# ScalarE scales keys and values of a chunked recurrence, and 24 gathered row sets change their stage

## The chip, the cores and the metric

The kernel runs on one core of one Trainium2 chip. The metric is the device time of one execution in microseconds. Three timed runs of the kernel before gave 5598.96, 5606.19 and 5611.48 us; the median is 5606.19.

## The reference

One layer of a hybrid trunk for 128 context tokens and 512 latent tokens, model width 2048, all in float32:

```python
h = rmsnorm(x, norm_mix) * (1 + sc1) + sh1          # modulated by m = silu(cond) @ w_mod + b_mod
q, k, v = silu(short_conv(h @ w_in[qkv]))           # 8 heads of 128; q and k of unit norm
# gated delta rule, forward and backward in time:
# S_t = exp(g_t) (I - beta_t k_t k_t^T) S_{t-1} + beta_t k_t v_t^T ;  o_t = S_t^T q_t / sqrt(dk)
p_a = (rmsnorm(o) * silu(z)) @ w_branch_a
p_b = chunk_spatial_gate(u, vg) @ w_branch_b        # one 128x128 position mix per channel group
x = x + gt1 * ((sigmoid(ga) * p_a + sigmoid(gb) * p_b) @ w_out)
h2 = rmsnorm(x, norm_ffn) * (1 + sc2) + sh2
# PEER: 8 heads, 2 x 128 sub-keys, top 16 of each half
s = (h2 @ w_query) . sub_keys
sv, si = top_k(s, 16)
cand = sv[0][:, None] + sv[1][None, :]              # 16 x 16 sums
best, pos = top_k(cand, 16); gates = softmax(best)
y = sum_e gelu(h2 . expert_u[idx_e]) * gate_e * expert_v[idx_e]      # 128 experts for each token
x = x + gt2 * y;  y_out = rmsnorm(x, norm_final)
```

The latent scans start from a cached state; the context's final states are an output.

## The kernel before, in words

Tokens go in five blocks of 128, one partition each: block 0 is the context, 1 to 4 the latent. The program is a row of stages, each a block with one instruction list per engine, and a barrier between them. `modulation` and `mixer_input` come first. Then the context goes through `qkv`, `deltanet`, `branches`, `merge`, `output_projection`, `expert_input` and `scores`; the four latent blocks go together through `qkv` and `deltanet`; then the second group (latent block 1) and the last group (blocks 2 to 4) each go through `branches` to `scores`; `experts` is last. Weights come in tiles of 1 MB over SyncE's queue into a ring of four.

**Row sets.** Each token has 128 chosen experts. The kernel takes them one place at a time: a row set is one row of 8 KB for each of the 128 tokens of a block, gathered by one indirect DMA of GpSimd (L316), 1 MB in all. A block needs 128 sets of `peer_u` and then 128 of `peer_v`; five blocks need 1280. VectorE uses a set in one instruction on 128x2048: a multiply and sum for `peer_u` (L363), a multiply and add into the block's total for `peer_v` (L368). Between both ScalarE applies Gelu once (`gelu_rows`). The context's sets are free for use once its `scores` are done, so they are spread over the stages that follow. `take(t, counts, slots)` names how many sets lie behind each step of a stage and in how many buffers; `use_rows` is VectorE's part, `gather_rows` and `gather_until` GpSimd's, which wait until a set's buffer has been used; `gather_ahead` issues the first three sets of the stage that follows. What is left is done by `experts` with six buffers, and nothing else is computed there. Before, 451 sets lie ahead of `experts` and 829 in it.

**The recurrence (`deltanet`).** A batch is one block of 128 tokens in one direction for all 8 heads: two batches for the context, eight for the latent. A triangular system is inverted by doubling in levels 1 to 6. In each level TensorE multiplies the masked matrix (L902), ScalarE copies the product from PSUM (L1107), TensorE multiplies again (L908), and VectorE adds the result into the inverse (L1038, L1040). GpSimd makes the mask product for each level (L838) in two buffers. Between levels VectorE also makes `kbe`, `kd` and `vn`, the transposed keys and values times a factor per token and head (L1051, L1053, L1056), after level 4 and 5 the decay terms of the next batch (L1001, L1013). TensorE puts products for the next batch behind its levels 4 and 5 (L892). After level 6 VectorE runs `begin` for the next batch (L1021 to L1030), then takes the outputs (L1072, L1074) and sums the state (L1077), for which TensorE waits before the next batch's transposes of the keys (L897). In the latent recurrence 4 row sets go with each of the first seven batches in three buffers: one after level 2, one after level 3, two after level 6.

**`branches`.** For each of 8 heads TensorE projects a z tile (L216) and transposes the head's normalised output (L1186), which GpSimd scales first (L1166) and then issues the gathers behind that head. Then come 2 x 4 tiles of `vg` (L1224), with most of the sets behind them, and 8 of `u`.

**`output_projection`.** 4 x 3 banks of products (L1500), each multiplied by VectorE (L1532) with sets behind it, and added to x by GpSimd (L1549). For the last group it also closes the context's block (L1512 to L1520) ahead of the first product.

**`scores`.** 16 tiles of queries (L216) and their scores (L1662). VectorE finds the top 16 of each (`top`), forms the 256 sums (L1725), finds their top 16 (L1732 to L1744) and picks the keys (`route`). All sets lie ahead of the first tile.

## Time and profile before

| | us |
|---|---|
| median of three runs | 5606.19 |
| profiled execution, its time | 5607.62 |
| its span | 5605.8 |
| VectorE busy | 3904.2 (70%) |
| TensorE matmul busy | 3073.4 (55%) |
| GpSimd busy | 2940.7 (52%) |
| ScalarE busy | 519.0 (9%) |
| DMA, mean rate | 338 GB/s, 1892.52 MB |

Busy time is summed over the whole span; each stage has its own limit, so the share of an engine over the span says little of one stage. PE is TensorE, PEld its weight loads, DVE is VectorE, ACT ScalarE, POOL GpSimd, SP SyncE. An entry in brackets behind an instruction is its engine's idle time just before it, and who ended it.

### The profile page before, as it was taken

How to read it: one execution, taken by the hardware profiler on the slowest of the kernel's cores; microseconds unless marked ns; L12 is line 12 of the kernel's file. 1: busy time of each engine (PE TensorE's matmuls, PEld its weight loads, DVE VectorE, ACT ScalarE, POOL GpSimd, SP SyncE). 2: the span in 40 equal slices, each digit the busy share in tenths (PEclk: the TensorE clock that was granted, in tenths of full speed). 3: DMA queues.
4: the chain of work that ended last, by engine and by line, in shares of the span. 5: the costliest groups of instructions: out<-in, count | busy, mean ns of one | idle time of the engine just before them, and what ended most of it. 6: DMA issues, size and time to landing. Idle time of an engine off the chain costs nothing. (4 is left out here: it accounts for less than half of the span.)

```text
span 5605.8 us, 41938 instructions
## 1 busy us (share of the span) xinstructions
PE 3073.4 (55%) x16118; PEld 2149.6 (38%) x16118; DVE 3904.2 (70%) x4330; ACT 519.0 (9%) x857; POOL 2940.7 (52%) x1532
## 2 busy tenths in 40 slices
PE   5989988998997886898998967000000000000000
PEld 2787955448996875455554444000000000000000
DVE  1340027976664436665776679899999999999998
ACT  1521002422221000000000000000000000000000
POOL 0131003745552210544543520888888888888887
PEclk7999989999999998999999988555555555555555
DMA  9819878973227996897999851999999999999998
GB/s 388 345 56 344 320 300 321 395 316 110 80 76 302 391 388 239 336 358 310 420 420 404 358 225 61 422 420 422 422 419 421 419 421 420 420 408 422 422 422 363
DMA packets 272942, 1892.52 MB, mean 338 GB/s; under 512 B 31780, under 2 KB 36132, under 8 KB 49511
## 3 DMA queue, kind: packets, MB, share of 16 engines
q0 software_dynamic: 194560, 1409.51, 61.5%
q1 hardware_dynamic: 71558, 440.26, 20.1%
q10 hardware_dynamic: 6624, 40.07, 1.8%
q8 instruction: 128, 2.10, 0.1%
q14 instruction: 72, 0.58, 0.0%
HBM read 1870.78 MB, written 18.94 MB: 337 GB/s over the span
## 5 line engine op out<-in xcount | busy, mean ns | idle before, releaser
L216 PE MATMUL ps<-arena_sb 128*128 128x128 f32 (+2 forms) x9216 | 1889.4, 367 | 128.4 <-PEq L1634 32.6
L316 POOL DMA_INDIRECT arena_sb<-peer_v,arena_sb x640 | 1303.6, 2037 | 840.5 <-DVE arena_sb L368 426.0
L368 DVE SCALAR_TENSOR_TENSOR arena_sb<-arena_sb 128x2048 f32<-128x2048 f32 x635 | 1497.8, 2359 | 193.7 <-DMA arena_sb<-peer_v,arena_sb 120.6
L216 PEld LDWEIGHTS ps<-arena_sb 128*128 128x128 f32 x9216 | 1328.9, 196 | 706.8 <-issue 324.4
L363 DVE CUSTOM_DVE_ANT_0 arena_sb<-arena_sb 128x2048 f32<-128x2048 f32 x640 | 1475.3, 2319 | 176.6 <-DMA arena_sb<-peer_u,arena_sb 176.3
L316 POOL DMA_INDIRECT arena_sb<-peer_u,arena_sb x640 | 1258.8, 1967 | 459.2 <-DVE arena_sb L363 266.9
L262 POOL DMA_DIRECT2D arena_sb<-w_mod x64 | 34.8, 544 | 617.3 <-PE ps L223 485.9
L838 POOL TENSOR_TENSOR arena_sb<-arena_sb 128x1024 f32<-128x1024 f32 x60 | 185.1, 3095 | 217.3 <-ACT arena_sb L1098 165.0
L1500 PE MATMUL ps<-arena_sb 128*128 128x512 f32 x640 | 279.4, 599 | 30.7 <-PEq L1354 30.0
L1419 DVE TENSOR_TENSOR arena_sb<-ps,arena_sb 128x128 f32<-128x128 f32 (+1 forms) x96 | 35.2, 378 | 350.4 <-PE ps L216 350.1
L908 PE MATMUL ps<-arena_sb 128*128 128x64 f32 x1760 | 206.4, 275 | 0.0
L908 PEld LDWEIGHTS ps<-arena_sb 128*128 128x128 f32 x1760 | 203.6, 194 | 0.0
L1500 PEld LDWEIGHTS ps<-arena_sb 128*128 128x128 f32 x640 | 122.7, 192 | 186.7 <-issue 184.3
L902 PE MATMUL ps<-arena_sb 128*128 128x128 f32 x1280 | 176.5, 292 | 10.8 <-DVE arena_sb L1030 9.4
L902 PEld LDWEIGHTS ps<-arena_sb 128*128 128x128 f32 x1280 | 163.9, 204 | 14.4 <-issue 9.8
L223 PE MATMUL ps<-arena_sb,scond_sb 128*32 128x512 f32 x768 | 129.5, 711 | 56.4 <-ACT scond_sb L436 30.1
L1224 PE MATMUL ps<-arena_sb 128*128 128x512 f32 x320 | 143.6, 607 | 11.4 <-DMA arena_sb<-w_vg 11.4
L1038 DVE TENSOR_TENSOR arena_sb<-arena_sb,ps 128x256 f32<-128x256 f32 x100 | 42.0, 420 | 146.8 <-PE ps L908 146.7
L1549 POOL TENSOR_TENSOR arena_sb<-arena_sb 128x512 f32<-128x512 f32 x20 | 41.9, 2093 | 194.6 <-DVE arena_sb L1532 194.4
L659 DVE TENSOR_SCALAR arena_sb<-ps,cw_sb 128x128 f32<-128x128 f32 (+1 forms) x48 | 26.4, 551 | 139.4 <-PE ps L216 138.3
L1841 ACT ACTIVATE ps<-arena_sb 128x2048 f32<-128x2048 f32 x4 | 7.5, 1882 | 1139.1 <-DVE arena_sb L1854 1139.1
L1403 ACT ACTIVATE arena_sb<-ps 128x128 f32<-128x128 f32 (+1 forms) x96 | 33.3, 348 | 803.1 <-PE ps L216 663.9
(222 smaller groups left out, 2299.9 us busy)
## 6 DMA issues: line engine op xcount, KB each, us to landing
arena_sb<-w_mod POOLq DMA_DIRECT2D x64, 1024.0 KB, 8.2
arena_sb<-w_qkv SPq DMA_DIRECT2D x48, 1024.0 KB
arena_sb<-w_ga SPq DMA_DIRECT2D x48, 1024.0 KB
arena_sb<-w_gb SPq DMA_DIRECT2D x48, 1024.0 KB
arena_sb<-w_out SPq DMA_DIRECT2D x48, 1024.0 KB
arena_sb<-w_query SPq DMA_DIRECT2D x48, 1024.0 KB
arena_sb<-w_mod SPq DMA_DIRECT2D x32, 1024.0 KB
arena_sb<-w_z SPq DMA_DIRECT2D x24, 1024.0 KB
```

The lines of the kernel that those rows point to most:

```text
L216: mm = pe.matmul(out, weights[:, k * P:(k + 1) * P], x[:, k, :], start=(k == 0), stop=(k == chunks - 1))
L223: mm = pe.matmul(out[32 * j:32 * j + 32, :], t.scond[:, k + j, :], weights[:, j * COL:(j + 1) * COL], start=start, stop=stop, tile_positio ...
L316: nc.gpsimd.indirect_dma_start(slot, None, a["peer_v" if adds else "peer_u"], bass.IndirectOffsetOnAxis(ap=g.index[:, p:p + 1], axis=0)).t ...
L363: nc.vector.tensor_tensor_reduce(rows, rows, total, 1.0, 0.0, ALU.mult, ALU.add, g.dots[:, p:p + 1]).then_inc(t.rows_used, 1)
L368: nc.vector.scalar_tensor_tensor(out=total, in0=rows, scalar=g.weight[:, p:p + 1], in1=total, op0=ALU.mult, op1=ALU.add).then_inc(t.rows_u ...
L838: nc.gpsimd.tensor_tensor(lev[:, k % 2], mt, over(nmask[:, 1 - r, k], H), ALU.mult).then_inc(s["level_masked"], 1)
L902: mm = pe.matmul(bank(out + u)[:, h % 4], lhs[:, h], rhs[:, h], start=True, stop=True)
L908: mm = pe.matmul(compact(bank(2 + u), k, side)[:, h % 4], lhs[:, h], changed(rhs, k, second)[:, h], start=True, stop=True)
L1038: nc.vector.tensor_tensor(cols, cols, compact(bank(2 + u), k, 1), ALU.add)
L1224: mm = pe.matmul(t.ps[:, 4 * c + b, :], h[:, k, b * P:(b + 1) * P], tile_slot(t, H + 4 * c + kq)[:, kk * COL:(kk + 1) * COL], start=(k == ...
L1500: mm = pe.matmul(t.ps[:, 4 * (c % 2) + b, :], merged[:, k, b * P:(b + 1) * P], tile_slot(t, 4 * c + kq)[:, kk * COL:(kk + 1) * COL], start ...
L1549: nc.gpsimd.tensor_tensor(cols, cols, part[:, b], ALU.add).then_inc(part_added, 1)
```

## The change

In `deltanet` the three multiplies by a factor per token and head leave VectorE; ScalarE makes each as 8 copies of 128x128 from PSUM with a scale operand, after the same level. TensorE waits for `kbe` by a semaphore of its own. The latent batches have 7 row sets each: two after levels 1, 2 and 3, one after level 5, none after level 6. GpSimd issues one gather after each of the masks 3 to 6 and three at the batch's end. In `branches` of the second and last group GpSimd issues gathers at the stage's start and then those behind head n-1 once it has scaled head n. In `output_projection` of the last group the closing of the context's block is a function called after the second column, and no set lies behind the last three products. In all `scores` stages the 16 x 16 sums become 4 x 16 and 12 x 4 (a sum of place i and j can only be among the best 16 if (i+1)(j+1) is at most 16), and the place is worked out in float steps; in the last group 10 sets are added between the heads. Lists of `take`: the last `branches` 76 to 75 sets, the last `output_projection` 38 to 32, the last `scores` 10 to 20, the latent recurrence 28 to 49; 475 sets lie ahead of `experts` and 805 in it.

```diff
+FULL = 4
+FEW = 4
+PAIRS = FULL * 16 + (16 - FULL) * FEW
@@ deltanet
-    behind = take(t, [4] * loads, 3, 6)
+    behind = take(t, [7] * loads, 3, 6)
@@ deltanet, gpsimd
                 for k in range(3, LEVELS):
                     masked(n, at[0], k)
-                    if n < loads and k >= 5:
-                        gather_until(pool, nc, t, a, min(behind[n].start + k - 1, t.rows))
+                    if n < loads:
+                        gather_until(pool, nc, t, a, min(behind[n].start + k + 1, t.rows))
...
-                    gather_until(pool, nc, t, a, min(behind[n].start + 7, t.rows))
+                    gather_until(pool, nc, t, a, min(behind[n].stop + 3, t.rows))
@@ deltanet, tensor
             def finish(n, r, j, b):
+                pe.wait_ge(s["kbe_done"], n + 1)
@@ deltanet, vector
                     level(n, r, k)
-                    if k == 1:
-                        dve.wait_ge(s["ktok_ps"], n + 1)
-                        nc.vector.tensor_tensor(kbe, banks(6), wide(gate(t.beg, r, b, 0, 8), P), ALU.mult)
-                    elif k == 2:
-                        nc.vector.tensor_tensor(kd, banks(6), wide(tail, P), ALU.mult)
-                    elif k == 3:
-                        dve.wait_ge(s["vtok_ps"], n + 1)
-                        nc.vector.tensor_tensor(vn, banks(0), wide(gate(t.beta, r, b, 0, 8), P),
-                                                ALU.mult).then_inc(s["tok_read"], 1)
-                    elif n + 1 < 2 * nb and k == 4:
+                    if n + 1 < 2 * nb and k == 4:
+                        dve.wait_ge(s["tok_read"], n + 1)
                         differences(n + 1, *order[n + 1])
...
-                    if n < loads and k in (2, 3):
-                        use_rows(dve, nc, t, behind[n][k - 2:k - 1])
-                if n < loads:
-                    use_rows(dve, nc, t, behind[n][2:4])
+                    if n < loads and k in (1, 2, 3, 5):
+                        use_rows(dve, nc, t, behind[n][6:7] if k == 5 else behind[n][2 * k - 2:2 * k])
@@ deltanet, scalar
+            def scaled(out, first, scales):
+                for h in range(H):
+                    ins = nc.scalar.activation(out[:, h], bank(first + h // 4)[:, h % 4], ACT.Copy,
+                                               scale=scales[:, h:h + 1])
+                return ins
...
+                    if k == 1:
+                        act.wait_ge(s["ktok_ps"], n + 1)
+                        scaled(kbe, 6, beg).then_inc(s["kbe_done"], 1)
+                    elif k == 2:
+                        scaled(kd, 6, tail)
+                    elif k == 3:
+                        act.wait_ge(s["vtok_ps"], n + 1)
+                        scaled(vn, 0, beta).then_inc(s["tok_read"], 1)
+                    if n < loads and k in (1, 2, 3, 5):
+                        gelu_rows(act, nc, t, behind[n][6:7] if k == 5 else behind[n][2 * k - 2:2 * k])
@@ branches
-                  [4, 3] * (H // 2) + [27] + [3] * (H - 1) + [0], 4)
+                  [3] * H + [30] + [3] * (H - 1) + [0], 4)
@@ branches, gpsimd
+            if not ctx:
+                gather_rows(pool, nc, t, a, [range(t.held, t.held)], 0)
             pool.wait_ge(o_step, 2 * nb + 2)
             for n in range(H):
...
-                else:
-                    gather_rows(pool, nc, t, a, behind, n)
+                elif n:
+                    gather_rows(pool, nc, t, a, behind, n - 1)
@@ output_projection
-    behind = take(t, [4, 3] * 5 + [3, 0] if last else [0] * (4 * nb), 4)
+    behind = take(t, [4, 4, 4, 4, 4, 4, 3, 3, 2, 0, 0, 0] if last else [0] * (4 * nb), 4)
@@ output_projection, vector
-            if last:
+            def finish_context():
...
                     use_rows(dve, nc, t, behind[nb * c + b])
+                if last and c == 1:
+                    finish_context()
@@ scores
-    behind = take(t, [0 if ctx else 10 if nb == 3 else 4], 4 if nb == 3 else 3)
+    behind = take(t, [10, 2, 1, 2, 1, 2, 1, 1, 0] if nb == 3 else [0 if ctx else 4] + [0] * H, 4 if nb == 3 else 3)
@@ scores, route
-                step.step(nc.vector.tensor_tensor(
-                    sums.rearrange("p b (i j) -> p b i j", i=TOPK),
-                    value[0].unsqueeze(3).to_broadcast([P, nb, TOPK, TOPK]),
-                    value[1].unsqueeze(2).to_broadcast([P, nb, TOPK, TOPK]), ALU.add))
+                for lo, hi, w, o in ((0, FULL, TOPK, 0), (FULL, TOPK, FEW, FULL * TOPK)):
+                    n = hi - lo
+                    ins = nc.vector.tensor_tensor(
+                        sums[:, :, o:o + n * w].rearrange("p b (i j) -> p b i j", i=n),
+                        value[0][:, :, lo:hi].unsqueeze(3).to_broadcast([P, nb, n, w]),
+                        value[1][:, :, 0:w].unsqueeze(2).to_broadcast([P, nb, n, w]), ALU.add)
+                step.step(ins)
...
+                step.step(nc.vector.tensor_copy(place_f, place))
+                at, by16, by4 = (place_f[:, u * n5:(u + 1) * n5] for u in range(3))
+                first, second = spot_f[:, 0:n5], spot_f[:, n5:2 * n5]
+                step.step(nc.vector.scalar_tensor_tensor(out=first, in0=by4, scalar=float(FULL - FULL * TOPK // FEW),
+                                                         in1=by16, op0=ALU.add, op1=ALU.max))
+                for out, w in ((down[0], TOPK), (down[1], FEW)):
+                    ins = nc.vector.scalar_tensor_tensor(out=out, in0=first, scalar=-float(w), in1=at, op0=ALU.mult,
+                                                         op1=ALU.add)
+                step.step(ins)
+                step.step(nc.vector.scalar_tensor_tensor(out=second, in0=down[1], scalar=float(FULL * FEW - FULL * TOPK),
+                                                         in1=down[0], op0=ALU.add, op1=ALU.max))
...
             for h in range(H):
                 top(2 * h)
                 top(2 * h + 1)
                 route(h)
+                use_rows(dve, nc, t, behind[h + 1])
```

## Rows read from the trace of the kernel before

**Rows 1.** The page: mean busy share of the DMA engines in 40 slices.

```profile
DMA  9819878973227996897999851999999999999998
```

**Rows 2.** Windows by stage: us, busy time (instructions) of each engine, clock, DMA share, GB/s.

```profile
1263.60:1719.70 456.10, 419.25 (x3520) 413.95 (x3520) 296.68 (x520) 111.13 (x192) 227.83 (x100) 0.95 0.23 82
1719.90:1854.20 134.30, 101.52 (x616) 79.09 (x616) 65.16 (x52) 15.33 (x28) 33.81 (x35) 0.95 1.00 416
2241.60:2542.90 301.30, 280.55 (x824) 154.18 (x824) 201.82 (x114) 18.26 (x29) 153.65 (x84) 0.96 0.87 342
3300.60:3496.80 196.20, 165.68 (x576) 101.79 (x575) 179.42 (x690) 9.65 (x18) 4.22 (x4) 0.93 0.25 91
3496.80:5605.80 2109.00, 0.00 (x0) 0.00 (x0) 1953.32 (x1236) 18.73 (x22) 1790.78 (x826) 0.50 1.00 416
```

**Rows 3.** Windows of the gathers (L316) alone in `experts`: GpSimd busy (instructions), clock, DMA.

```profile
4350.00:4900.00 550.00, 477.39 (x221) 0.50 1.01 420
```

**Rows 4.** Groups by line in the latent recurrence: busy us, mean ns, idle before.

```profile
L363 DVE CUSTOM_DVE_ANT_0 arena_sb<-arena_sb 128x2048 f32<-128x2048 f32 x28 | 64.8, 2333 | 0.0
...
L1056 DVE TENSOR_TENSOR arena_sb<-ps,beta_sb 128x1024 f32<-128x1024 f32 x8 | 9.7, 1218 | 0.0
```

**Rows 5.** TensorE in time order at a batch's start, context then latent, and one window.

```profile
352.92 1.09 PE L897 MATMUL ps<-ident_sb,arena_sb 128*128 128x128 f32 x8 [0.51 <-DVE arena_sb L1077]
353.84 1.95 PE L902 MATMUL ps<-arena_sb 128*128 128x128 f32 x16
...
1449.82 1.97 PE L897 MATMUL ps<-ident_sb,arena_sb 128*128 128x128 f32 x8 [3.74 <-DVE arena_sb L1077]
1451.58 3.62 PE L902 MATMUL ps<-arena_sb 128*128 128x128 f32 x16
...
1449.70:1455.00 5.30, 5.18 (x25) 5.18 (x25) 0.07 (x1) 0.60 (x1) 5.07 (x3) 0.50 0.51 206
```

**Rows 6.** VectorE and GpSimd in time order in a latent batch, and the gathers' landing.

```profile
1461.13 2.36 POOL L838 TENSOR_TENSOR arena_sb<-arena_sb 128x1024 f32<-128x1024 f32 x1 [3.50 <-PE ps L902]
1462.82 0.42 DVE L1038 TENSOR_TENSOR arena_sb<-arena_sb,ps 128x256 f32<-128x256 f32 x1 [1.85 <-PE ps L908]
...
1466.66 4.26 POOL L838 TENSOR_TENSOR arena_sb<-arena_sb 128x1024 f32<-128x1024 f32 x1 [3.17 <-PE ps L902]
...
arena_sb<-peer_u,arena_sb POOLq DMA_INDIRECT x28, 6.1
```

**Rows 7.** VectorE in time order: the state sums of the first and seventh latent batch.

```profile
1338.11 1.20 DVE L1077 TENSOR_TENSOR arena_sb<-arena_sb,ps 128x1024 f32<-128x1024 f32 x1
...
1672.23 1.21 DVE L1077 TENSOR_TENSOR arena_sb<-arena_sb,ps 128x1024 f32<-128x1024 f32 x1
```

**Rows 8.** Groups by line and form, ScalarE, whole span: instructions on 128x128.

```profile
L1690 ACT ACTIVATE arena_sb<-ps 128x128 f32<-128x128 f32 x32 | 8.9, 277 | 150.1 <-PE ps L216 150.1
...
L713 ACT ACTIVATE arena_sb<-ps,small_sb 128x128 f32<-128x128 f32 x16 | 5.9, 367 | 19.8 <-PE ps L600 19.8
```

**Rows 9.** Last `branches`: a wait (us in total, times, longest), and the first `vg` products.

```profile
PE ps L1186 <- POOL arena_sb L1166: 14.3, 5, 4.0
...
2349.64 50.79 PE L1224 MATMUL ps<-arena_sb 128*128 128x512 f32 x114
```

**Rows 10.** Last `output_projection` in time order: start, us, instruction.

```profile
3066.36 166.97 PE L1500 MATMUL ps<-arena_sb 128*128 128x512 f32 x384 [17.43 <-PEq L1354]
...
3248.92 0.68 DVE L1532 TENSOR_TENSOR arena_sb<-ps,arena_sb 128x512 f32<-128x512 f32 x1
...
3253.60 0.94 POOL L316 DMA_INDIRECT arena_sb<-peer_v,arena_sb  x1 [0.30 <-issue]
...
3263.87 0.17 DVE L1581 TENSOR_REDUCE stat_sb<-stat_sb 128x3 f32<-128x12 f32 x1 [14.27 <-PEq L1447]
```

**Rows 11.** Last `scores`, groups by line and form.

```profile
L1716 DVE MAX8 arena_sb<-arena_sb 128x8 f32<-128x128 f32 x48 | 10.9, 282 | 0.6
...
L1725 DVE TENSOR_TENSOR arena_sb<-arena_sb 128x768 f32<-128x768 f32 x8 | 7.7, 959 | 0.3
L1741 DVE MAX8 arena_sb<-arena_sb 128x8 f32<-128x256 f32 x24 | 8.6, 415 | 0.3
```

More of the change, by code:

```diff
@@ L1103, in _ @@
             for n in range(2 * nb):
+                r, _, b = order[n]
+                beg, beta = (x[:, g.first + b, 8 * r:8 * r + 8] for x in (t.beg, t.beta))
                 for k in range(1, LEVELS):
@@ L1486, in _ @@
                     gelu_rows(act, nc, t, behind[nb * c + b])
+                if last and c == 1:
+                    act.wait_ge(fin_step, 2)
+                    nc.scalar.activation(x_c, total, ACT.Square, accum_out=ss_c).then_inc(fin_root, 1)
+                    act.wait_ge(fin_step, 3)
+                    nc.scalar.activation(ss_c, ss_c, ACT.Sqrt).then_inc(fin_root, 1)
             act.wait_ge(norm_in, 48)
@@ L1534, in _ @@
                     use_rows(dve, nc, t, behind[nb * c + b])
+                if last and c == 1:
+                    finish_context()
                 if c == 2:
@@ L1616, in scores @@
     z = g.scratch
-    value = [z[:, u * n5:(u + 1) * n5].rearrange("p (b n) -> p b n", b=nb) for u in range(2)]
-    keyf = [z[:, (2 + u) * n5:(3 + u) * n5].rearrange("p (b n) -> p b n", b=nb) for u in range(2)]
-    where = z[:, 4 * n5:5 * n5].bitcast(U32).rearrange("p (b n) -> p b n", b=nb)
-    place = [z[:, (5 + u) * n5:(6 + u) * n5].bitcast(U32) for u in range(3)]
-    place_f = [z[:, (8 + u) * n5:(9 + u) * n5] for u in range(2)]
-    o = 10 * n5
-    sums = z[:, o:o + nb * 256].rearrange("p (b n) -> p b n", b=nb)
-    left = z[:, o + nb * 256:o + 2 * nb * 256].rearrange("p (b n) -> p b n", b=nb)
-    onehot = [z[:, o + (2 + u) * nb * 256:o + (3 + u) * nb * 256] for u in range(2)]
+    part_of = lambda i, w=1: z[:, i * n5:(i + w) * n5]
+    value = [part_of(u).rearrange("p (b n) -> p b n", b=nb) for u in range(2)]
+    where = part_of(2).bitcast(U32).rearrange("p (b n) -> p b n", b=nb)
+    place, place_f = part_of(3, 3).bitcast(U32), part_of(6, 3)
+    spot_f, down = part_of(9, 2), [part_of(11), part_of(12)]
+    keyf = [[part_of(13 + 2 * s + u).rearrange("p (b n) -> p b n", b=nb) for u in range(2)] for s in range(2)]
+    o = 17 * n5
+    sums = z[:, o:o + nb * PAIRS].rearrange("p (b n) -> p b n", b=nb)
+    left = z[:, o + nb * PAIRS:o + 2 * nb * PAIRS].rearrange("p (b n) -> p b n", b=nb)
+    onehot = z[:, o + 2 * nb * PAIRS:o + 2 * nb * (PAIRS + 256)]
     total = t.stat[:, 0:nb * H]
@@ L1652, in _ @@
             else:
-                gather_rows(pool, nc, t, a, behind, 0)
+                gather_rows(pool, nc, t, a, behind, H)
                 gather_ahead(pool, nc, t, a)
@@ L1690, in _ @@
                 nc.scalar.activation(query[n % 2], t.ps[:, n % 4, 0:nt], ACT.Copy).then_inc(query_done, 1)
+                if n % 2 and n > 4:
+                    gelu_rows(act, nc, t, behind[n // 2 - 1])
+            for rows in behind[H - 1:]:
+                gelu_rows(act, nc, t, rows)
             if ctx:
@@ L1720, in top @@
                 step.step(ins)
-                step.step(nc.vector.tensor_copy(keyf[u], where))
+                step.step(nc.vector.tensor_copy(keyf[n // 2 % 2][u], where))
             def route(h):
-                step.step(nc.vector.tensor_tensor(
-                    sums.rearrange("p b (i j) -> p b i j", i=TOPK),
-                    value[0].unsqueeze(3).to_broadcast([P, nb, TOPK, TOPK]),
-                    value[1].unsqueeze(2).to_broadcast([P, nb, TOPK, TOPK]), ALU.add))
+                for lo, hi, w, o in ((0, FULL, TOPK, 0), (FULL, TOPK, FEW, FULL * TOPK)):
[5 more added lines that the diff above has]
+                step.step(ins)
                 best = best_all[:, :, h, :]
-                spot = place[0].rearrange("p (b k) -> p b k", b=nb)
+                spot = place[:, 0:n5].rearrange("p (b k) -> p b k", b=nb)
                 for b in range(nb):
@@ L1745, in route @@
                 step.step(ins)
[L1746 to L1754 removed]
+                nc.vector.tensor_scalar(place[:, n5:2 * n5], place[:, 0:n5], 4, None, ALU.logical_shift_right)
```

30 lines of the change are left out of this document (12 added, 18 removed).

## The prediction

> **What bounds the kernel now.** I read the slices of the page first: over the last two fifths the DMA digits stand at 9 without a break, and before that they fall to 2 to 7 in places [rows 1]. The windows by stage say more [rows 2]. The last 2109 us (`experts`) hold no matmul and run at 416 GB/s with a DMA share of 1.00, VectorE 1953 us busy. What sets the pace there is the gather of row sets (128 rows of 8 KB, 1.0486 MB): 221 in 550 us of steady run at 420 GB/s [rows 3], 2.49 us each. VectorE takes 1953/829 = 2.36 us of that. So a row set used earlier gives back 2.49 us at the end, and the question for each earlier stage is what it pays. Those stages have other limits [rows 2]: the latent recurrence has TensorE 419 of 456 us busy with a DMA share of 0.23; `branches` of the last group 281 of 301; `scores` of the last group has VectorE 179 of 196 and DMA 0.25.
>
> **Row sets moved.** Summing the `take` lists (those of 128x1 stages are unchanged): recurrence 28 to 49, last `branches` 76 to 75, last `output_projection` 38 to 32, last `scores` 10 to 20. Net 24 sets leave `experts`: 24 x 2.49 = -59.8 us. The whole stage, its ends included, gives 2109/829 = 2.54, so the term lies between -59 and -61.
>
> **The recurrence.** Per batch VectorE loses three multiplies of 1.22 us and gains three row sets [rows 4]. Before, two sets lie at the batch's end, between level 6 and `begin`. TensorE waits there for the state sum: 3.74 us idle, then the clock stands at 0.50, 1.2 GHz, for some 5 us: 8 transposes take 1.97 us and level 1's first 16 products 3.62 [rows 5]. The context's batches have no sets there and show what it is like without: 0.51 us idle, 1.09 and 1.95 us for the same. So taking both sets away is worth 3.2 of idle time and 0.9 + 1.7 of slow products, 5.8 us a batch.
> What it costs: a level takes 5.5 us; between the adds of two levels VectorE has its multiply of 1.22 and 1.85 us idle [rows 4, 6], 3.1 in all, and some 0.8 more before TensorE wants the next columns: about 3.9. Two sets take 4.42, so TensorE slips 0.6 us a level. Beyond that there are two further prices. First, GpSimd's mask multiply takes 2.36 us alone and 4.26 beside a set [rows 6]; the two exclude each other. With two sets in a row the mask can go between them: VectorE's pair then takes 6.8 us and TensorE slips 2.9. The Trainium skill (SBUF — State Buffer, "SBUF: two separate sides") has the rule: a VectorE instruction with two SBUF inputs and a GpSimd one hold the shared port pair for a whole instruction, and the other is blocked; the 1.9 us added beside a set agree. By the rule each level pays the 2.9, by no contention the 0.6. Second, only three buffers: sets 0 to 2 are there, set 3 is issued behind mask 3 and once set 0 is used, and lands 6.1 us after issue [rows 6]. Following GpSimd's order from the state sum (0): set 3 issues at 10 to 12 and lands at 16 to 18 (wanted 15.5), set 4 lands at 22 (wanted 21), set 5 at 26 to 29 (wanted 23). Level 4's adds come at 28 to 31; two blocks of 16 products for the next batch (1.95 each, as level 1's) stand between level 4 and 5 and cover most. Level 6 then starts at 37.3 to 39.2 instead of 36.5 (33.7 without slips). A batch comes to 53.7 to 55.5 us against 55.7 (six periods between the ends of these state sums, 1339.31 to 1673.44 [rows 7]). I take 55.0: 7 batches x -0.7 = -5 us. Ends: -2.6 a batch (no contention, timely landings) and +3 (each landing 2 us later, another mask in the way): -18 to +20.
> ScalarE's 8 multiplies of 128x128 from PSUM: 277 ns as a plain one, 367 with a pointer operand [rows 8]; 8 x 0.367 = 2.9 us (at least 2.2, and 3.7 if the scale costs a second 90 ns). Between a level's copies and the next level's it is idle as long as a level less its two copies, 5.5 - 1.6 = 3.9 us. I count nothing; if that cover fails by x us, TensorE waits x three times a batch. The table load for Gelu falls here once: 3 us either way, and it leaves a later stage.
>
> **`branches` of the last group.** GpSimd scales head n+1 only after the gathers behind head n, and these wait for VectorE. TensorE waits 14.3 us for it in five places, and some tiles after a wait run slower; eight heads take from 2241.6 [rows 2] to 2349.6 [rows 9], 108 us. A tile without a wait takes 11.0 us with its transposes, as in `scores` (sixteen from 3287.9 to 3466). With the gathers one head behind, GpSimd has scaled a head some 12 us before it is wanted, VectorE's part being 0.6 + 3 x 2.45 = 8 us: 13.5 for the first tile at the slow clock + 7 x 11.0 + 0.5 = 91. DMA then carries 3 sets and a tile in 11 us, 381 GB/s, under 422 but near. I take -14 (ends -6 and -17). The three sets more behind the `vg` products (30) cost nothing: 30 x 2.45 = 73 us beside 117 us of TensorE. In the stage of the second group the early gather changes nothing: DMA share is 1.00 all through.
>
> **`output_projection` of the last group.** Products end at 3233.3, but VectorE, with sets behind each product, is at its last one at 3248.92; GpSimd then issues the three gathers ahead (last 3253.60) and the next stage starts at 3263.87 [rows 10]. In the change all sets lie behind the first nine products. VectorE, waiting for landings, does a set in 3.4 us here, so 12 sets from 3103 to 3145, 12 more to 3186, the moved closing of the context 11 us, 8 sets to 3223: just before the tenth product's 3226.5. The moved closing saves nothing where it was: its wait for loads from the ScalarE queue lay before the first product was ready. Last product at 3234, last gather 3239, next stage 9.3 us later as now, 3248.7: -15. Ends: -17, and -8 if VectorE arrives 7 us late.
>
> **`scores`.** Candidates fall from 256 to 112. A maximum takes 415 ns at 256 and 282 at 128, 1.04 ns an element, so 265 at 112 [rows 11]; I take the index search and the replacement at the same rate. Per head with three blocks that is 15 x -0.15, and -0.3 for the sums (336 elements for 768, in two instructions): -2.6 us. The index arithmetic goes from 4 small instructions (0.64 us) to 7: +0.75. 8 x -1.9 = -15. Ten sets more at 2.45: +24.5. VectorE is the one behind: TensorE's last product ends at 3466, the stage at 3496.8 [rows 2]. So +9 (ends +4 and +14). With one block the same is -0.1 a head: -1 for each of the two other stages, -2 together (ends -3 and +6, if the added steps wait longer).
>
> **Sum.** -59.8 - 5 - 14 - 15 + 9 - 2 = -86.8. The profiled execution took 5607.6 (span 5605.8 and 1.8 around it), so 5520.8; it lies 1.4 above the median of the runs, so 5519.
>
> **Rivals.** (a) The recurrence pays: every level gives the full contention and landings are late, +3 a batch. For it: 4.26 beside a set [rows 6]. Against: 3.9 us cover and the products between level 4 and 5. +20 instead of -5: 5544.
> (b) The two stage gains don't come, since DMA stands near its limit there: `branches` at 381 of 422 GB/s, and `output_projection` has fewer sets but denser. -6 and -8 instead of -14 and -15, and with it +14 in `scores`: 5539. Against: what VectorE waits for is set by the order of GpSimd's program, not by bytes.
> (c) It goes better: landings in time and 5.8 us a batch mostly kept, -18 for it, and -17 twice: 5501.
> (d) Slower than before: with three buffers the gathers become the batch's chain. Sets 3, 4, 5 and 6 each expose landing and use, 6.1 + 2.3 = 8.4 us, and since GpSimd sits in a gather's wait its masks come late too, so that nothing covers: 33.6 - 5.8 = +28 a batch, +195 for seven: 5519 + 5 + 195 = 5719. It decides from (86.8 - 5)/7 = 11.7 us a batch on. Against: no mask needs a set that needs that mask, and the sets wanted first have landed.
>
> **Numbers.** Forecast 0.60, (a) 0.16, (b) 0.13, (c) 0.08, (d) 0.03. What a measurement here can tell from no change is 0.2%, 11 us; same and slower lie only in (d) or several ends together: faster 0.95, same 0.02, slower 0.03. Range: all good ends give 5495, all bad ones but (d) 5572; 8 in 10 lie in 5492 to 5555.
>
> **What would show it.** In `experts` 805 sets and some 2049 us; if it isn't 60 shorter, the first term is wrong. In the latent recurrence: TensorE's idle before L897 under 1 us and the clock at 2.4 GHz there; waits of the second set of levels 2 and 3 for peer rows; a period of 54 to 56. If TensorE waits for ScalarE copies or for masks (POOL L838), my covers were wrong. In `branches` the 14 us wait for POOL gone and eight heads in 91 to 100 us. In `output_projection` the last product read within 1 us of 3233's counterpart. In `scores` 205 us. The forecast is wrong if the recurrence takes over 480 us, or if a stage between grows by what `experts` loses.

## The result, and the profile after

The changed kernel takes 5573.64 us (median of 4 runs, 5569.33 to 5587.77) beside 5607.51 for the kernel before (4 runs, 5598.96 to 5611.48): a ratio of 0.9946, 95% interval 0.9924 to 0.9968. It is faster, since the interval leaves out 1, but by 34 us and not by the forecast's 87; 5519 was 55 us too low and the range ended 19 us under the median. The profiled execution is the slowest of the four, 5587.77 (span 5585.9), so it lies 19.8 us under the profiled one of before, and the table accounts for that difference.

| stage, start to next start, us | before | after | change | forecast |
|---|---|---|---|---|
| latent recurrence | 456.3 | 505.6 | +49.3 | -5 |
| last `branches` | 310.6 | 308.5 | -2.0 | -14 |
| last `output_projection` | 197.5 | 184.6 | -13.0 | -15 |
| last `expert_input` and `scores` | 233.4 | 242.2 | +8.8 | +9 |
| the other two `scores` | 179.5 | 177.0 | -2.5 | -2 |
| `experts` | 2108.5 | 2047.5 | -61.0 | -59.8 |
| all others | 2119.0 | 2119.6 | +0.6 | 0 |

The same stages in the windows of the trace after (columns as in [rows 2]): recurrence, last `branches`, last `output_projection`, last `scores`, `experts`.

```profile
1263.80:1769.20 505.40, 452.14 (x3520) 445.70 (x3520) 352.48 (x520) 163.69 (x387) 270.69 (x121) 0.88 0.33 117
2287.90:2596.40 308.50, 276.13 (x825) 153.28 (x826) 197.89 (x133) 18.16 (x29) 146.69 (x83) 0.94 0.85 337
3111.60:3296.20 184.60, 166.42 (x384) 73.43 (x384) 94.92 (x50) 12.16 (x28) 86.73 (x44) 0.95 0.82 330
3334.50:3538.40 203.90, 165.72 (x576) 101.79 (x574) 186.74 (x724) 9.66 (x18) 20.29 (x14) 0.91 0.37 141
3538.40:5585.90 2047.50, 0.00 (x0) 0.00 (x0) 1896.66 (x1212) 18.73 (x22) 1739.91 (x802) 0.50 1.00 416
```

Beside [rows 2], TensorE's matmuls in the recurrence are the same 3520, but busy 452 us instead of 419, and the granted clock's mean is 0.88 instead of 0.95: the products themselves ran longer. That splits the 49 us: 33 are slower products, the other 16 more idle time (505.4 - 452.1 = 53.3 us beside 456.1 - 419.3 = 36.9). `experts` keeps its 416 GB/s and is shorter only by what it no longer does.

TensorE's idle time in the recurrence by what it waited for (us in total, times, longest), the kernel before and then the changed one:

```profile
PE ps L897 <- DVE arena_sb L1077: 26.2, 7, 3.7
```

```profile
PE ps L905 <- DVE arena_sb L1044: 25.9, 16, 4.5
PE ps L905 <- POOL arena_sb L841: 13.0, 2, 8.2
PE ps L900 <- DVE arena_sb L1071: 3.9, 7, 0.9
```

The wait for the state sum fell from 26.2 to 3.9 us as forecast. In its place came 25.9 us of waits for VectorE's adds (L1044) and 13.0 us for GpSimd's masks (L841), of which the kernel before had 0.7. The six periods between the ends of the first seven state sums are 57.2 to 65.1 us, 62.0 on the mean, against 55.7 before and 55.0 forecast; the stretch from the stage's start to the first of them grew from 75.7 to 88.8.

One latent batch of after, TensorE in time order, from the end of the batch before (start, us, instruction, idle before):

```profile
1469.68 1.09 PE L900 MATMUL ps<-ident_sb,arena_sb 128*128 128x128 f32 x8 [0.51 <-DVE arena_sb L1071]
1470.61 1.95 PE L905 MATMUL ps<-arena_sb 128*128 128x128 f32 x16
1472.40 3.74 PE L911 MATMUL ps<-arena_sb 128*128 128x64 f32 x32
1475.98 2.17 PE L905 MATMUL ps<-arena_sb 128*128 128x128 f32 x16
1477.98 3.68 PE L911 MATMUL ps<-arena_sb 128*128 128x64 f32 x32
1483.77 3.75 PE L905 MATMUL ps<-arena_sb 128*128 128x128 f32 x16 [2.10 <-DVE arena_sb L1044]
1487.32 6.93 PE L911 MATMUL ps<-arena_sb 128*128 128x64 f32 x32
```

VectorE and GpSimd in the same stretch:

```profile
1476.85 3.89 DVE L366 CUSTOM_DVE_ANT_0 arena_sb<-arena_sb 128x2048 f32<-128x2048 f32 x1
...
1480.67 2.28 DVE L366 CUSTOM_DVE_ANT_0 arena_sb<-arena_sb 128x2048 f32<-128x2048 f32 x1
...
1484.21 4.15 DVE L366 CUSTOM_DVE_ANT_0 arena_sb<-arena_sb 128x2048 f32<-128x2048 f32 x1
...
1488.71 5.04 DVE L366 CUSTOM_DVE_ANT_0 arena_sb<-arena_sb 128x2048 f32<-128x2048 f32 x1 [0.34 <-DMA arena_sb<-peer_u,arena_sb]
```

```profile
1476.23 2.36 POOL L841 TENSOR_TENSOR arena_sb<-arena_sb 128x1024 f32<-128x1024 f32 x1
1481.02 2.80 POOL L319 DMA_INDIRECT arena_sb<-peer_u,arena_sb  x1 [2.43 <-DVE arena_sb L366]
1483.82 2.38 POOL L841 TENSOR_TENSOR arena_sb<-arena_sb 128x1024 f32<-128x1024 f32 x1
1486.36 2.85 POOL L319 DMA_INDIRECT arena_sb<-peer_u,arena_sb  x1 [0.16 <-issue]
1489.23 2.36 POOL L841 TENSOR_TENSOR arena_sb<-arena_sb 128x1024 f32<-128x1024 f32 x1
```

The batch's start is as forecast: 0.51 us idle, transposes 1.09 and level 1's products 1.95, against 3.74, 1.97 and 3.62 in [rows 5]. Then come two sets in a row. Beside a mask (L841) a set takes 3.9 to 5.0 us instead of 2.3, and the gather's issue (L319) takes 2.8 us instead of 0.94 [rows 10] when it runs beside a set. TensorE waits 2.10 us for the adds (L1044) behind the second set, and what follows runs at half the clock: level 3's products take 3.75 and 6.93 us where level 1's take 1.95 and 3.74. The clock shows it, 1.00 in the window of levels 1 and 2 and 0.50 in that of level 3:

```profile
1470.00:1482.00 12.00, 11.67 (x104) 11.44 (x101) 6.57 (x7) 6.51 (x20) 9.48 (x6) 1.00 0.65 249
1483.80:1494.20 10.40, 10.40 (x48) 10.25 (x48) 10.06 (x8) 3.25 (x10) 10.05 (x5) 0.50 0.61 203
```

The longest wait for a mask, 8.20 us, has a cause of its own. It falls in the fifth batch, the first one of the backward direction, whose start state SyncE loads from memory once the last forward batch is done:

```profile
1530.42 0.38 SPq L825 DMA_DIRECT2D arena_sb<-state  x1
...
1541.19 2.69 POOL L862 TENSOR_TENSOR arena_sb<-arena_sb 128x1024 f32<-128x1024 f32 x1 [9.56 <-issue]
...
1550.63 3.79 PE L905 MATMUL ps<-arena_sb 128*128 128x128 f32 x16 [8.20 <-POOL arena_sb L841]
```

These 512 KB land 10.7 us after their issue, among the gathers of the batch's end (5.9 us in the kernel before). GpSimd's first multiply of the batch (L862) waits for them by the program, and its masks come behind that. The kernel before has the same load, but no wait of TensorE for a mask in this batch.

### The profile page after: what moved, and what is told of

Read it like the earlier page. It is cut to its first block and busy times, and to the rows that moved or that the text cites. A ratio compares the mean times of both kernels' runs of the same rounds, so it can differ in the third digit from the quotient of the medians.

```text
span 5585.9 us, 42233 instructions
## 1 busy us (share of the span) xinstructions
PE 3098.4 (55%) x16118; PEld 2175.9 (39%) x16118; DVE 3880.2 (69%) x4372; ACT 581.4 (10%) x1097; POOL 2930.9 (52%) x1532
## 5 line engine op out<-in xcount | busy, mean ns | idle before, releaser
L319 POOL DMA_INDIRECT arena_sb<-peer_v,arena_sb x640 | 1277.9, 1997 | 926.3 <-DVE arena_sb L371 556.1
L371 DVE SCALAR_TENSOR_TENSOR arena_sb<-arena_sb 128x2048 f32<-128x2048 f32 x635 | 1513.7, 2384 | 247.9 <-DMA arena_sb<-peer_v,arena_sb 178.0
L366 DVE CUSTOM_DVE_ANT_0 arena_sb<-arena_sb 128x2048 f32<-128x2048 f32 x640 | 1499.8, 2359 | 167.3 <-DMA arena_sb<-peer_u,arena_sb 166.6
L219 PEld LDWEIGHTS ps<-arena_sb 128*128 128x128 f32 x9216 | 1319.9, 194 | 716.5 <-issue 332.9
L319 POOL DMA_INDIRECT arena_sb<-peer_u,arena_sb x640 | 1291.8, 2018 | 480.0 <-DVE arena_sb L366 289.8
L841 POOL TENSOR_TENSOR arena_sb<-arena_sb 128x1024 f32<-128x1024 f32 x60 | 163.7, 2736 | 224.4 <-ACT arena_sb L1092 182.1
L911 PE MATMUL ps<-arena_sb 128*128 128x64 f32 x1760 | 227.4, 292 | 0.0
L911 PEld LDWEIGHTS ps<-arena_sb 128*128 128x128 f32 x1760 | 225.0, 210 | 0.0
L905 PE MATMUL ps<-arena_sb 128*128 128x128 f32 x1280 | 186.9, 304 | 49.6 <-DVE arena_sb L1044 25.9
L1515 PEld LDWEIGHTS ps<-arena_sb 128*128 128x128 f32 x640 | 122.8, 193 | 187.6 <-issue 184.5
L905 PEld LDWEIGHTS ps<-arena_sb 128*128 128x128 f32 x1280 | 173.1, 215 | 54.5 <-issue 38.6
L1549 DVE TENSOR_TENSOR arena_sb<-ps,arena_sb 128x512 f32<-128x512 f32 x20 | 13.8, 688 | 157.2 <-PE ps L1515 157.2
```

What stands on the lines that cost most here:

```text
L219: mm = pe.matmul(out, weights[:, k * P:(k + 1) * P], x[:, k, :], start=(k == 0), stop=(k == chunks - 1))
L319: nc.gpsimd.indirect_dma_start(slot, None, a["peer_v" if adds else "peer_u"], bass.IndirectOffsetOnAxis(ap=g.index[:, p:p + 1], axis=0)).t ...
L366: nc.vector.tensor_tensor_reduce(rows, rows, total, 1.0, 0.0, ALU.mult, ALU.add, g.dots[:, p:p + 1]).then_inc(t.rows_used, 1)
L371: nc.vector.scalar_tensor_tensor(out=total, in0=rows, scalar=g.weight[:, p:p + 1], in1=total, op0=ALU.mult, op1=ALU.add).then_inc(t.rows_u ...
L841: nc.gpsimd.tensor_tensor(lev[:, k % 2], mt, over(nmask[:, 1 - r, k], H), ALU.mult).then_inc(s["level_masked"], 1)
L905: mm = pe.matmul(bank(out + u)[:, h % 4], lhs[:, h], rhs[:, h], start=True, stop=True)
```

## The experiments

Each of these runs but e9 is one execution. They are compared by their stages, since two executions differ by some 10 us elsewhere (`modulation` alone took from 123 to 130 us). The recurrence itself repeats well: e8 has that of the changed kernel and took 504.8 us beside 505.6, e9 has that of e7 and took 463.1 beside 463.0. First the window of the latent recurrence of e1, e2, e3, e4, e5, e6, e7 and e10, in this order; the stage's length is the number before the comma.

```profile
1258.20:1715.70 457.50, 418.19 (x3520) 413.11 (x3520) 272.57 (x496) 160.67 (x385) 215.16 (x100) 0.95 0.23 81
```

```profile
1256.30:1684.40 428.10, 407.85 (x3520) 401.95 (x3520) 280.49 (x496) 160.84 (x384) 207.23 (x100) 0.98 0.25 87
```

```profile
1255.70:1721.90 466.20, 430.86 (x3520) 424.90 (x3520) 297.93 (x521) 163.56 (x388) 166.26 (x122) 0.93 0.35 127
```

```profile
1262.30:1758.20 495.90, 440.38 (x3520) 433.77 (x3520) 361.91 (x544) 114.48 (x196) 269.54 (x121) 0.91 0.34 119
```

```profile
1263.00:1749.00 486.00, 445.98 (x3744) 438.44 (x3744) 346.32 (x521) 164.29 (x388) 270.43 (x121) 0.96 0.34 122
```

```profile
1260.80:1710.00 449.20, 416.99 (x3520) 410.34 (x3520) 329.35 (x513) 165.96 (x387) 237.34 (x114) 0.96 0.34 116
```

```profile
1261.80:1724.80 463.00, 421.55 (x3520) 415.35 (x3520) 340.76 (x520) 165.07 (x387) 245.55 (x121) 0.95 0.37 128
```

```profile
1259.50:1723.30 463.80, 418.23 (x3520) 411.39 (x3520) 378.64 (x544) 116.31 (x196) 232.96 (x121) 0.96 0.36 128
```

**e1: ScalarE's scaling alone.** The changed kernel with four sets a batch, placed and gathered as before.

```diff
-    behind = take(t, [7] * loads, 3, 6)
+    behind = take(t, [4] * loads, 3, 6)
+    CUT = (0, 0, 1, 2, 2, 2, 4)
...
+    use_rows(dve, nc, t, behind[n][CUT[k - 1]:CUT[k]])
```

> The changed kernel, but the latent recurrence has its 4 row sets a batch where they were before (one after level 2, one after level 3, two after level 6) and GpSimd's gathers as before; ScalarE keeps the scaling. Recurrence before 456 us, changed 505. If the row sets' number and place make the 49 us (theories A and B below): 448 to 458 us, VectorE only relieved. If ScalarE's scaling makes them (theory C: its 24 short instructions delay the copies TensorE waits for): 480 us or more, with waits of TensorE for L1109 copies. Theory A: two sets in a row on VectorE and GpSimd's masks and gathers shut each other out for whole instructions, the levels slip, and TensorE's idle time drops its clock. Theory B: with three buffers the sets land late and VectorE waits for them.

5587.52 us; the recurrence takes 457.5 beside 456.3 before. Moving the scaling neither costs nor gains anything while the sets stand where they stood. The 49 us come with the sets' new number and places.

**e2: four sets, apart.** Against e1 (GpSimd's gathers follow, one behind each of the masks 3 to 6):

```diff
-    CUT = (0, 0, 1, 2, 2, 2, 4)
+    CUT = (0, 1, 2, 3, 3, 4, 4)
```

> As the run before, but the 4 sets of a batch go one after each of levels 1, 2, 3 and 5, none after level 6. A and B both expect that the 5.8 us a batch of idle and slow TensorE at the batch's start go; A takes back up to 0.8 us in each of three levels (set 2.3 + mask 2.35 against 3.9 us of cover), so 416 to 432 us for the recurrence (456 before); B nothing, 416. C: 480 or more. Fewer sets early (28 for 49) cost 21 x 2.49 = 52 us in experts.

5555.41 us, the recurrence 428.1, and five of the six periods between its first seven state sums are 50.8 us (the fourth is 53.9). With the clock at 0.98 and TensorE 408 of 428 us busy this is nearly TensorE's own time. Against e1 that is 29 us, 4.2 a batch: two sets of 2.3 us taken off the end of a batch, where nothing hid them. The forecast's gain of 5.8 a batch for this came to 4.5 in the periods (55.3 to 50.8).

**e3: the masks nearly taken away.** GpSimd multiplies only 8 of the 128 columns of each mask; the buffers are cleared once, so the rest is zero and most of the masked matrix is left out.

```diff
-                nc.gpsimd.tensor_tensor(lev[:, k % 2], mt, over(nmask[:, 1 - r, k], H),
+                nc.gpsimd.tensor_tensor(lev[:, k % 2, :, 0:8], mt[:, :, 0:8], over(nmask[:, 1 - r, k, 0:8], H),
                                         ALU.mult).then_inc(s["level_masked"], 1)
```

> The changed kernel with 7 sets, but each of GpSimd's mask products is made on 8 of 128 columns only (the rest of the buffer is cleared once), so the solve leaves most of its levels' mask out. Waits and order are unchanged. A: the sets on VectorE fall from 2.3 to 5.0 us back to 2.3 to 2.4 beside masks (gathers can still stretch one), 7 us a batch: recurrence 450 to 465 us, TensorE at the full clock in level 3 and 4. B: the landings stay where they are, sets wait longer instead: 495 to 505 us.

5541.06 us, the recurrence 466.2 (1 us over theory A's range): 39 of the 49 us are gone. The groups by line of e3's recurrence:

```profile
L366 DVE CUSTOM_DVE_ANT_0 arena_sb<-arena_sb 128x2048 f32<-128x2048 f32 x30 | 74.2, 2488 | 12.1 <-DMA arena_sb<-peer_u,arena_sb 12.1
L319 POOL DMA_INDIRECT arena_sb<-peer_u,arena_sb x30 | 44.5, 1484 | 17.8 <-DVE arena_sb L366 12.3 <-issue 5.1
...
L371 DVE SCALAR_TENSOR_TENSOR arena_sb<-arena_sb 128x2048 f32<-128x2048 f32 x18 | 42.3, 2349 | 11.0 <-DMA arena_sb<-peer_v,arena_sb 10.4
```

and of the changed kernel's:

```profile
L366 DVE CUSTOM_DVE_ANT_0 arena_sb<-arena_sb 128x2048 f32<-128x2048 f32 x30 | 95.1, 3181 | 14.3 <-DMA arena_sb<-peer_u,arena_sb 14.3
L319 POOL DMA_INDIRECT arena_sb<-peer_u,arena_sb x30 | 55.1, 1838 | 12.8 <-DVE arena_sb L366 7.3 <-issue 4.8
L371 DVE SCALAR_TENSOR_TENSOR arena_sb<-arena_sb 128x2048 f32<-128x2048 f32 x18 | 58.8, 3266 | 15.3 <-DMA arena_sb<-peer_v,arena_sb 15.1
```

A set falls from 3.2 to 2.4 us on the mean. The waits for landings, 22.5 and 29.4 us, are 7 apart, so they aren't what the 39 us were. The edit does two things at once, though: it frees the sets, and it brings the masks themselves earlier, for which TensorE waits 4.5 us here and 13.0 in the changed kernel. Up to some 8.5 of the 39 us can be that.

**e4: seven sets, VectorE scales.** The three multiplies of 1.22 us a batch put back ahead of the sets, and ScalarE's taken away.

```diff
+                    if k == 1:
...
+                        nc.vector.tensor_tensor(kbe, banks(6), wide(gate(t.beg, r, b, 0, 8), P), ALU.mult)
+                    elif k == 2:
+                        nc.vector.tensor_tensor(kd, banks(6), wide(tail, P), ALU.mult)
+                    elif k == 3:
...
+                        nc.vector.tensor_tensor(vn, banks(0), wide(gate(t.beta, r, b, 0, 8), P),
+                                                ALU.mult).then_inc(s["tok_read"], 1)
```

> The changed kernel with 7 sets, but keys and values are scaled by VectorE as before (three multiplies of 1.22 us between the levels). A and B: VectorE's chain between levels is what sets the time, so 3 x 1.2 us more a batch: recurrence 505 + 26 = 525 to 535 us. C: ScalarE's part was the cost, 456 to 495 us.

5579.87 us, the recurrence 495.9: 10 us less than with ScalarE's scaling, some 30 under what A and B had and 1 us past C's range. It fits none of them well: C blamed ScalarE's instructions for the whole 49, and e1 had cleared them. VectorE and one mask in time order:

```profile
1468.85 1.22 DVE L1054 TENSOR_TENSOR arena_sb<-ps,beg_sb 128x1024 f32<-128x1024 f32 x1
1469.99 2.74 DVE L366 CUSTOM_DVE_ANT_0 arena_sb<-arena_sb 128x2048 f32<-128x2048 f32 x1
...
1476.19 1.21 DVE L1056 TENSOR_TENSOR arena_sb<-ps,stat_sb 128x1024 f32<-128x1024 f32 x1
1477.33 3.01 DVE L366 CUSTOM_DVE_ANT_0 arena_sb<-arena_sb 128x2048 f32<-128x2048 f32 x1
```

```profile
1468.22 2.36 POOL L841 TENSOR_TENSOR arena_sb<-arena_sb 128x1024 f32<-128x1024 f32 x1
```

The first set of levels 1 and 2 takes 2.74 and 3.01 instead of 3.89 and 4.15: while VectorE multiplies from PSUM, GpSimd's mask runs at its full speed (2.36 us, from 1468.22 on) and is nearly done when the set starts. So the multiply costs 1.2 us and gives 1.15 back, and the change's own edit removed a help. That reading rests on these rows; no run took it apart further, and what else makes up the 10 us isn't shown.

**e5: TensorE kept busy in the waits.** Eight products of the identity with itself ahead of levels 3 and 4, into a bank that is overwritten.

```diff
+    if not ctx and n < loads and k in (3, 4):
+        for i in range(8):
+            pe.matmul(bank(4)[:, i % 4], t.ident[:], t.ident[:], start=True, stop=True)
```

> The changed kernel, and in the latent recurrence TensorE multiplies the identity with itself eight times (into a PSUM bank that the next product overwrites) ahead of the products of levels 3 and 4 of each batch with sets: this fills idle time of the changed kernel and adds some 0.5 to 1 us of work a time. Theory A (beside the wait itself, each idle stretch of 2 to 4 us costs TensorE's clock: after it the 16 + 32 products of a level took 3.7 + 6.9 us instead of 2.0 + 3.7): the granted clock of the stage rises from 0.88 to 0.93 or more, the products behind the filled waits take their short times, and the latent recurrence falls from 505.6 to 475 to 492 us. Theory B (the waits for VectorE are the whole cost and the slow products are hidden beside VectorE's sets): the stage stays at 503 to 512 us whatever the clock does. The kernel by A: 5555 to 5573 us; by B: 5585 to 5595.

5572.72 us, the recurrence 486.0: work added, 19.6 us less in the stage (the kernel 15 less, since its last `branches`, which the edit leaves alone, took 5.6 us longer). Level 3 in time order (L935 is the filling):

```profile
1478.36 2.00 PE L935 MATMUL ps<-ident_sb 128*128 128x128 f32 x16
1480.54 2.05 PE L905 MATMUL ps<-arena_sb 128*128 128x128 f32 x16 [0.18 <-DVE arena_sb L1047]
1482.43 3.74 PE L911 MATMUL ps<-arena_sb 128*128 128x64 f32 x32
```

The products behind the wait take 2.05 and 3.74 again and the mean clock is 0.96. Each of the eight has two records, and the waits for VectorE's adds fell too, from 25.9 to 17.4 us in all. That is 8.5 of the 19.6 us; the rest goes with the clock, which is thus a price of its own, beside the wait that brings it. The 8.2 us wait for a mask in the fifth batch stands here too, and that batch still takes 65.6 us: the filling stands behind the wait for the mask.

**e6 and e7: six and seven sets, apart.** One after each of levels 1, 2, 3 and 5, one in level 4 ahead of the decay differences, one behind the state sum; in e7 one more after level 6.

```diff
                     if n + 1 < 2 * nb and k == 4:
+                        if n < loads:
+                            use_rows(dve, nc, t, behind[n][3:4])
                         dve.wait_ge(s["tok_read"], n + 1)
                         differences(n + 1, *order[n + 1])
...
                 nc.vector.tensor_tensor(st, st2, banks(6), ALU.add).then_inc(s["batch_done"], 1)
+                if n < loads:
+                    use_rows(dve, nc, t, behind[n][CUT[6]:])
```

> The changed kernel with six sets a batch in place of seven, none two in a row: one after each of levels 1, 2, 3 and 5, one in level 4 ahead of the decay differences (where VectorE waits 2.2 us for ScalarE with four sets a batch) and one behind the state sum (where it waits 4.8 us). 42 sets in the recurrence. Theory A (what lengthens the batches is where the sets stand: two in a row outlast TensorE's level, one does not): 50.8 us a batch as with four sets apart, plus 0 to 2.5 us for the two more, the latent recurrence 428 to 445 us; `experts` 812 sets, 2065 us; the kernel 5519 to 5537 us. Theory B (VectorE and GpSimd together have too much to do with more than some four sets, wherever they stand): 2.3 to 3.5 us more a batch for each set over four, 460 to 477 us, the kernel 5551 to 5568 us.

> As the kernel with six apart, with the seventh set after level 6: the same 49 sets in the recurrence as in the changed kernel, in other places. Theory A (place, not number): the set after level 6 stands on TensorE's path and costs its 2.3 us a batch, the others little; 50.8 + 2.3 to 5 us a batch, the latent recurrence 444 to 463 us, `experts` as in the changed kernel (2047.5 us), the kernel 5525 to 5545 us. Theory B (number): near the changed kernel, 485 to 510 us in the recurrence, the kernel 5566 to 5592 us.

e6: 5548.84 us, the recurrence 449.2; e7: 5544.54 us and 463.0, with the very same 49 sets as the changed kernel in 42.6 us less. So the place makes most of the 49 us. The number isn't free either: e6 missed theory A's 445 by 4 and its 5537 by 12, while its `experts` came as told (2065.2). From e2 to e7 the same kind of placing takes 21 sets more and 34.9 us more, 1.7 a set, where a set gives back 2.49 in `experts`; what is left is 17 us and not 52.

The fifth batch stands out in all of these runs (53.9 us in e2, 59.9 in e6, 61.1 in e7, 65.2 in e9 and e10). It is the batch of the start state again: in e7 the load is issued at 1509.00 and lands 7.5 us later, GpSimd's first multiply starts at 1516.58, and TensorE then waits 7.1 us for a mask. The gathers pass from `peer_u` to `peer_v` in the same batch in e6 and e7, but in e2 they don't and the batch is long all the same. No run moved the load.

**e8: 26 sets behind `vg`.**

```diff
-    [3] * H + [30] + [3] * (H - 1) + [0], 4)
+    [3] * H + [26] + [3] * (H - 1) + [0], 4)
```

> The changed kernel with 26 in place of 30 sets behind the `vg` products of the last `branches`; four more sets go to `experts`. Theory A (the sets behind `vg` take 3.35 us each because their gathers share the queues with the weights of `vg`, so VectorE reaches the `vg` scaling late and TensorE waits 13.9 us for it): the wait falls to 0 to 3 us, the stage from 308.5 to 294 to 298 us, `experts` gains 10 us, the kernel 5582 to 5587 us beside 5587.8. Theory B (the stage is bound by its bytes from HBM, not by that wait): the time moves to the next wait, the stage loses less than 5 us and the kernel is 5 to 10 us longer.

5575.33 us. Last `branches` takes 294.1 (-14.4), `experts` 2056.8 (+9.2). TensorE in time order at the end of `vg`, the changed kernel and then e8:

```profile
2492.89 0.80 PE L1209 MATMUL ps<-arena_sb 128*128 128x128 f32 x2 [13.92 <-DVE arena_sb L1300]
```

```profile
2473.13 0.49 PE L1209 MATMUL ps<-arena_sb 128*128 128x128 f32 x2 [1.94 <-DVE arena_sb L1300]
```

The wait fell by 12.0 us and the stage by 14.4, as theory A had it; the net of the edit is 5 us. The kernel's time is 7 us under theory A's range, by stages that the edit leaves alone.

**e9: both corrections.** The edits of e7 and e8 in one kernel.

> The changed kernel with both corrections together: the seven sets of a batch apart (as in the run with seven apart) and 26 in place of 30 sets behind `vg`. If the two are independent: recurrence 463 us, the last `branches` 294 us, `experts` 2057 us, the kernel 5544.5 - 5 = 5540 us, 5534 to 5546 us; a ratio to the kernel before of 0.988 (0.986 to 0.990). If the gathers of the one disturb the other: over 5550 us.

5533.72 us, median of 4 runs (5528.67 to 5541.8), beside 5609.97 for 7 runs of the kernel before: ratio 0.9866, 95% interval 0.9850 to 0.9883. The interval lies clear of the changed kernel's 0.9924 to 0.9968, so this version beats both. The stages are those of e7 and e8, each by itself: recurrence 463.1, last `branches` 294.3, `experts` 2057.1.

**e10: e7 with VectorE's scaling**, by e4's edit.

> The kernel with seven sets apart, but VectorE scales keys and values again, as in the kernel before, ahead of the sets after levels 1, 2 and 3 (three multiplications of 1.22 us a batch). Theory A (with the sets apart there is room beside TensorE in each level only for a set or for a set and 1.2 us, and ScalarE's taking the scaling is what makes it): a set of 2.3 to 3.1 us and 1.2 us outlast the level's free 4.3 us by 0 to 1 us, so 0 to 2 us a batch more than with ScalarE's scaling: the recurrence 463 to 477 us, the kernel 5545 to 5559 us. Theory B (with the sets apart ScalarE's part is worth its whole 3.7 us a batch): 489 to 493 us, the kernel 5570 to 5575 us. Theory C (as with seven in the old places, where VectorE's scaling let the mask run ahead of the sets and was worth 10 us): 453 to 462 us, under 5545 us.

5542.89 us, the recurrence 463.8 beside 463.0. The stage lies at the low end of theory A's range and the kernel's time in C's. VectorE is 38 us busier (378.64 us for 340.76) and TensorE no later: with the sets apart it makes no difference who scales.

## Why the prediction was wrong, point by point

**The step that failed: "Two sets take 4.42, so TensorE slips 0.6 us a level", and with it "A batch comes to 53.7 to 55.5 us".** The batches took 57.2 to 65.1 us, 62.0 on the mean. The room was right: in e2 a set of 2.7 to 3.2 us behind a level's adds fits and TensorE doesn't wait. The slip was not. Two things were priced too low. A pair takes 6.2 us at level 1 (3.89 + 2.28) and 9.2 at level 2 (4.15 + 5.04), since the second collides as well: with the next mask, which comes as soon as the slow gather is issued, and with that gather. My worst case was one collision a pair, 6.8. TensorE's waits for these adds came to 25.9 us. And I priced the idle time of TensorE at its own length, though [rows 5], which I used for what goes away, showed 3.74 us of idle followed by slow products. The same happened behind each new wait: 2.10 us idle brought 5.0 us of slower products (3.75 + 6.93 beside 1.95 + 3.74); over the stage the same 3520 products took 33 us more. e5 takes away 20 us, a part of the waits and a part of the slow products. e3 takes away 39, the collisions with the masks and the masks' own length. They overlap, since without the collisions most waits don't arise. e7 puts the whole together: the same sets, none two in a row, 463.0. The forecast's own sign of being wrong, a recurrence over 480 us, came true at 505.6. Rival (a) had the mechanism's first half and a size of +20 for the stage; it came to +49.

**A wait that no term had.** TensorE stands 8.2 us for a mask in the fifth batch, behind the load of the backward direction's start state. The forecast counted seven like batches, and named a wait for masks only as a sign that its covers were wrong.

**Landings** were the second price I named. VectorE waited 14.3 + 15.1 us for them, but e3 kept 12.1 + 10.4 of these and lost most of the cost: a minor part.

**ScalarE's part**, counted at nothing: right for ScalarE's own instructions. It is 3 x 64 instructions like these (a group of the recurrence after); TensorE never waits for one, e1 stands 1 us from before, and e10 1 us from e7. What the forecast didn't have is that VectorE's multiplies helped where they stood ahead of a pair: e4 is 10 us shorter with them.

```profile
L1096 ACT ACTIVATE arena_sb<-ps,beta_sb 128x128 f32<-128x128 f32 x64 | 17.3, 390 | 0.0
```

**`branches`, -14: the first half right, the sum not.** The waits for GpSimd's scaling are gone and eight heads take 87.7 us (2287.98 to 2375.69), 20 less than before; the forecast had 91, since it took 11.0 us for a head without a wait, and one takes 10.65 (the pitch of the seven behind the first). "The three sets more behind the `vg` products (30) cost nothing: 30 x 2.45 = 73 us beside 117 us of TensorE" failed. Two windows of the `vg` stretch of after:

```profile
2376.00:2426.00 50.00, 50.00 (x118) 22.06 (x117) 35.38 (x16) 2.64 (x4) 25.70 (x16) 1.00 1.00 410
2426.00:2476.00 50.00, 50.00 (x132) 24.78 (x131) 35.28 (x15) 3.07 (x4) 28.58 (x15) 1.00 1.01 413
```

15 to 16 sets in 50 us at a DMA share of 1.00, with the `vg` weights on the same DMA engines: 3.2 us a set. That is some 97 us for 30, beside 103 in which TensorE has products (2375.69 to 2478.97) and not the 117 that I took, and VectorE has work of its own there; it comes late to the scaling, and TensorE stands 13.92 us. The kernel before had 1.13 us of that wait already, in a row I hadn't read:

```profile
2455.67 0.49 PE L1195 MATMUL ps<-arena_sb 128*128 128x128 f32 x2 [1.13 <-DVE arena_sb L1286]
```

Of the 20 us that the first half gained, the second gave back 18; e8 shows 14 of them by taking the wait off.

**The other terms were right**: `experts` -61.0 for -59.8 (the rate of the end stage, 2.49 us a set, holds: e1 and e2 have 21 sets more there and 52 us more), `output_projection` -13.0 for -15, `scores` +8.8 and -2.5 for +9 and -2. In the last `scores` a maximum at 112 candidates takes 265 ns, as told; in `output_projection` VectorE takes the last product within 0.1 us of its end (3278.16), but the next stage starts 12.4 us after the last gather and not 9.3, for which I have no cause. Of the 67 us between the forecast's -87 and the profiled -20, 54 are the recurrence and 12 `branches`.

## What to carry to other kernels

A filler on a helper engine is worth first its place and then its time: put one piece in each gap of the bounding engine's dependency loop and never two in a row, and look at what the neighbour engine runs beside it. Even then price it: here a set in a gap of its own cost 1.7 us of the stage against 2.49 given back. Look through the loop for the one round that is unlike the others, such as the one that loads a new state. When you add a wait to TensorE, add the slow products behind it, by the rows in which the same trace shows that. And when fillers ride on a stage with its own loads, take their duration from the DMA share of that stage, not from the engine.

## What the runs showed of the hardware

- A short idle stretch can halve TensorE's granted clock: in the batch shown, 2.10 us idle, then 0.50 (1.2 GHz) through at least 10.4 us. Not each one does: e7's 1.77 us ahead of the transposes of a batch left the 13 us behind it at 1.00, and the clock fell only after these, for some 3 us. With products of no use in the gap (e5) the products behind it took their short times, the stage's mean was 0.96 instead of 0.88, and the stage was 19.6 us shorter for 224 more products in the records. The window in e7 (columns as above):

```profile
1454.20:1467.20 13.00, 11.98 (x104) 11.74 (x104) 8.04 (x13) 6.51 (x20) 10.49 (x5) 1.00 0.52 194
```

- Not only GpSimd's arithmetic collides with VectorE's sets: the issue of an indirect gather takes 2.80 us instead of 0.94 [rows 10] when it starts 0.35 us into a set, and ends 0.87 us after the set (1483.82 and 1482.95). With sets apart (e2) the issue for `peer_u` takes 1.08 us on the mean, in the changed kernel 1.84. The Trainium skill (SBUF — State Buffer, "SBUF: two separate sides") says that GpSimd can't write the descriptors of a DMA that it issues while VectorE holds the shared port pair; it says it of VectorE's two-port modes, and here the instruction beside the issue is a plain float32 instruction with two SBUF inputs.
- A VectorE multiply of 1.22 us that reads PSUM and one small operand from SBUF left GpSimd's mask beside it at 2.36 us, its time alone, and the set behind it was 1.15 us shorter (e4, 2.74 for 3.89): an instruction added to the fuller engine cost next to nothing.
- A load of 512 KB by SyncE landed 10.7 us after its issue in the changed kernel, where gathers were issued at 1528.15, 1529.43 and 1530.69 around its own 1530.42. It took 5.9 us in the kernel before (gathers at 1500.57 and 1502.65, the load at 1506.26) and 3.7 in e2 (no gather in the 6 us before it). That the gathers are what delays it is not shown by a run of its own.
